# Recurrence of a two-block network: products with the values issued ahead of their waits, and constant products between the steps of a triangular inverse

## The reference, cut to what matters

```python
def first_block(x, ...):
    x = x + FFN_HALF * swiglu(rms_norm(x, norm_ffn1[l]), ...)
    h = rms_norm(x, norm_mix[l])
    p = h @ w_in[l]
    sb_q, sb_k, sb_v, rw_in = jnp.split(p, [...], axis=-1)
    ...
    o_sb = stick_breaking_attention(q, k, v)
    o_sb = rms_norm(o_sb, sb_out_norm[l].reshape(SB_HEADS, HEAD_DIM)).reshape(B, S, SB_WIDTH)
    o_rw = rwkv7_time_mix(rw_in, ...)      # y = rwkv7_recurrence(r, heads(decay), kf, v, -kk, kk * a)
    x = x + jnp.concatenate([o_sb, o_rw], axis=-1) @ w_out[l]
    x = x + FFN_HALF * swiglu(rms_norm(x, norm_ffn2[l]), ...)
```

## Time and profile before

| | |
|---|---|
| time, median of 3 runs | 1114.93 us (1114.87, 1114.93, 1120.08) |
| time of the profiled execution | 1117.52 us |
| its span in the trace | 1115.7 us, so 1.8 us lie around it |
| PE busy | 1088.8 us, 98% of the span |
| DVE, ACT, POOL busy | 670.3, 448.1, 35.6 us |
| chain that ended last | PE 89%, DVE 6%, ACT 4% |
| mean granted TensorE clock | 0.987 of full speed |

### The profile page before, as it was taken

How to read it: one execution, slowest core, us unless ns; L and a number is a source line. 1 busy time by engine, 2 the same in 40 slices (tenths; PEclk the granted TensorE clock), 3 DMA queues, 4 the chain that set the end, 5 groups by cost and what they waited for, 6 DMA issues and landing times.

```text
span 1115.7 us, 19112 instructions
## 1 busy us (share of the span) xinstructions
PE 1088.8 (98%) x8212; PEld 896.2 (80%) x8212; DVE 670.3 (60%) x848; ACT 448.1 (40%) x573; POOL 35.6 (3%) x29
## 2 busy tenths in 40 slices
PE   9999999999998999999999999999999999999997
PEld 8999998999987669999998999989899753434343
DVE  6488777789554666777775573277559552222123
ACT  6333334864522244333335332267584521211112
POOL 0000000000430000000003000000000000000000
PEclk9999999999978999999999999999999999999999
DMA  9977756354200248598873353332356979999994
GB/s 333 390 257 238 251 188 206 119 175 148 90 2 2 76 140 314 190 337 295 306 265 114 96 184 110 108 118 104 114 192 264 375 319 402 422 410 419 422 418 201
DMA packets 121012, 254.29 MB, mean 228 GB/s; under 512 B 6241, under 2 KB 91505, under 8 KB 109426
## 3 DMA queue, kind: packets, MB, share of 16 engines
q1 hardware_dynamic: 119890, 250.54, 61.6%
q10 hardware_dynamic: 1056, 2.79, 0.8%
HBM read 252.25 MB, written 1.06 MB: 227 GB/s over the span
## 4 chain that ended last, share of the span: by engine, by line
PE 89%; DVE 6%; ACT 4%; issue 1%; DMA 0%; SPq 0%; ACTq 0%; DVEq 0%
PE ps L825 53%; PE ps L772 33%; ACT arena L1563 2%; DVE ring_r L2130 1%; ACT arena_r L1563 1%; DVE ring_r L2263 1%; PE ps L1308 1%; DVE arena L2451 1%; DVE arena L2317 1%; DMA x<-in_x 0%; DVE arena L2332 0%; PE ps L793 0%; ACT gb_r L1563 0%; PE ps L1513 0%; PE ps L781 0%
## 5 line engine op out<-in xcount | busy, mean ns | idle before, releaser
L825 PE MATMUL ps<-hall_r,arena_r 128*128 128x256 f32 x1632 | 299.6, 281 | 0.0
L825 PE MATMUL ps<-arena_r 128*128 128x256 f32 (+1 forms) x1216 | 284.4, 323 | 0.0
L2130 DVE TENSOR_TENSOR ring_r<-ring,arena_r 128x2048 fp32r<-128x2048 f32 x88 | 203.1, 2312 | 109.1 <-ACT arena_r L1563 106.6
L825 PEld LDWEIGHTS ps<-hall_r,arena_r 128*128 128x128 f32 x1632 | 252.8, 188 | 1.2 <-issue 0.3
L1563 ACT ACTIVATE arena_r<-ring 128x2048 fp32r<-128x2048 f32 (+1 forms) x101 | 191.1, 1899 | 150.3 <-PE ps L825 139.9
L825 PE MATMUL ps<-hall_r,ring_r 128*128 128x256 f32 x816 | 227.9, 279 | 0.0
L825 PEld LDWEIGHTS ps<-arena_r 128*128 128x128 f32 x1216 | 202.7, 188 | 18.9 <-issue 0.7
L772 PE MATMUL ps<-arena 64*64 64x32 f32 (+7 forms) x1944 | 195.8, 331 | 11.2 <-ACT arena L1563 5.0
L1563 ACT ACTIVATE arena<-ps 128x512 f32<-128x512 f32 (+3 forms) x136 | 80.4, 605 | 312.6 <-PE ps L825 186.2
L772 PEld LDWEIGHTS ps<-arena 128*64 128x64 f32 (+3 forms) x1944 | 117.8, 154 | 71.1 <-issue 58.6
L825 PEld LDWEIGHTS ps<-hall_r,ring_r 128*128 128x128 f32 x816 | 154.9, 190 | 0.9
(11 more groups left out here) (273 smaller groups left out, 1137.8 us busy)
## 6 DMA issues: line engine op xcount, KB each, us to landing
ring<-in_w_in SPq DMA_DIRECT2D x35, 1024.0 KB, 5.2
arena<-in_w_exp_down SPq DMA_DIRECT2D x32, 1024.0 KB, 11.8
ring<-in_ffn_up SPq DMA_DIRECT2D x22, 1024.0 KB, 5.3
ring<-in_ffn_down SPq DMA_DIRECT2D x22, 1024.0 KB, 5.0
ring<-in_ffn_gate SPq DMA_DIRECT2D x21, 1024.0 KB, 5.7
arena<-in_w_mod SPq DMA_DIRECT2D x18, 1024.0 KB, 9.3
arena<-in_w_exp_up SPq DMA_DIRECT2D x16, 1024.0 KB, 14.5
ring<-in_w_exp_gate SPq DMA_DIRECT2D x16, 1024.0 KB, 11.4
```

The source lines that it names most:

```text
L825: m = pe.matmul(out_, w[i], h[j], start=start and i + j == 0, stop=stop and j == 1, skip_group_check=group)
L2130: tt(lo(n), slot(n), hi(n), ALU.subtract).then_inc(S("w_lo"), 1)
```

## The change

The products of the recurrence that need only the values are split from the others. For chunk 0 the right side (`rec_rhs_v(0)`) is issued before the attention's mean squares; for the others it is issued at the end of the chunk before. The state's products with the values are issued in the wait for ACT's copy (for chunk 0 in the wait for DVE's), those of y in the wait for DVE's copy (for chunk 0 in the wait for the inverse). The state's sums move from bank 4 to bank 7. Two constant products of 128x128 weights with 256 columns (`keep_running`) are added at five places of the inverse, and one such product twice in a chunk. ACT copies `rhs_z` of chunk 0 before it copies the attention's output and takes the root. DVE's `sb_out(c)` comes after the state of chunk c, and the fourth after chunk 3. `rhs_z` moves from arena block 20 to block 4, and POOL clears its block and that of `u_z` by two commands that wait on earlier events.

```diff
-        rhs_z, u_z = (A(j).rearrange("p (q n) -> p q n", q=2) for j in (20, 21))
+        rhs_z, u_z = (A(j).rearrange("p (q n) -> p q n", q=2) for j in (4, 21))
...
-            pool.wait_ge(*W("inv_x", 5))
-            pool.memset(A(20, 2048), 0.0).then_inc(S("u_zero"), 1)
+            pool.wait_ge(*W("sb_z", 4))
+            pool.memset(A(4), 0.0).then_inc(S("u_zero"), 1)
+            pool.wait_ge(*W("inv_x", 4))
+            pool.memset(A(21), 0.0).then_inc(S("u_zero"), 1)
...
+            def rec_rhs_v(c):
+                for h in range(8):
+                    m = mm(ps[rec_rows(c), 0, h * CH:(h + 1) * CH], ak_t[:, 8 * (c // 2) + h, :],
+                           vz[:, c % 2, c // 2, h * HD:(h + 1) * HD], start=h == 0, stop=c == 0, group=True)
+                if c == 0:
+                    m.then_inc(S("rec_rhs"), 1)
+
+            def rec_rhs_state(c):
+                for h in range(8):
+                    m = mm(ps[rec_rows(c), 0, h * CH:(h + 1) * CH], arz[:, h % 2, h // 2, c, 0, :],
+                           state[:, c % 2, h // 2, :], start=False, group=True)
+                m.then_inc(S("rec_rhs"), 1)
+
+            def rec_state_v(c):
+                for h in range(8):
+                    o = ps[(h % 2) * HD:(h % 2 + 1) * HD, 7, (h // 2) * HD:(h // 2 + 1) * HD]
+                    mm(o, k_tok[:, c // 2, h * HD:(h + 1) * HD],
+                       vz[:, c % 2, c // 2, h * HD:(h + 1) * HD], start=h < 2, stop=False, group=True)
+
+            def rec_state_u(c):
+                for h in range(8):
+                    o = ps[(h % 2) * HD:(h % 2 + 1) * HD, 7, (h // 2) * HD:(h // 2 + 1) * HD]
+                    m = mm(o, b_tok[:, c // 2, h * HD:(h + 1) * HD],
+                           u_z[:, c % 2, h * HD:(h + 1) * HD], start=False, group=True)
+                m.then_inc(S("rec_state"), 1)
+
+            def rec_y_v(c):
+                if c >= 2:
+                    pe.wait_ge(*W("y_kept", c - 1))
+                for h in range(8):
+                    mm(rec_y_at(c, h), vz[:, c % 2, c // 2, h * HD:(h + 1) * HD],
+                       rk_t[:, 8 * (c // 2) + h, :], start=h < 2, stop=False, group=True)
+
+            def rec_y_u(c):
+                for h in range(8):
+                    m = mm(rec_y_at(c, h), u_z[:, c % 2, h * HD:(h + 1) * HD],
+                           rb_t[:, 8 * (c // 2) + h, :], start=False, stop=c == 0, group=True)
+                if c:
+                    for h in range(8):
+                        m = mm(rec_y_at(c, h), state[:, c % 2, h // 2, :], arz[:, h % 2, h // 2, c, 1, :],
+                               start=False, group=True)
+                m.then_inc(S("rec_y"), 1)
+
+            def keep_running():
+                for i in range(2):
+                    mm(ps[:, 7, 0:256], zeros[:, 0:P], zeros)
+
...
             inv_sums(1)
+            keep_running()
             inv_update(1)
+            keep_running()
             inv_sums(2)
+            keep_running()
             inv_update(2)
             sb_sums_a(0)
             sb_sums_a(1)
             inv_sums(3)
+            keep_running()
             inv_update(3)
...
             inv_sums(5)
             pe.wait_ge(*W("sb_expo", 4))
+            pe.wait_ge(*W("rec_masked", 3))
+            rec_rhs_v(0)
             pe.wait_ge(*W("sbo_sq", 2))
             four(4, lambda o, k: mm(o, head_mean, sq[:, k, :]), "sbo_ms")
+            keep_running()
             inv_update(5)
...
             for c in range(NCH):
...
                 if c:
                     pe.wait_ge(*W("state", c))
...
+                    rec_rhs_state(c)
+                if 0 < c < NCH - 1:
+                    rec_state_v(c)
+                if c == 0:
+                    pe.wait_ge(*W("sb_kept", 1))
+                    rec_y_v(c)
+                    pe.wait_ge(*W("tt_added", 5))
                 pe.wait_ge(*W("rhs_kept", c + 1))
...
                 m.then_inc(S("rec_u"), 1)
+                if c == 0:
+                    rec_state_v(c)
+                else:
+                    rec_y_v(c)
+                mm(ps[:, 6, 0:256], zeros[:, 0:P], zeros)
                 pe.wait_ge(*W("u_kept", c + 1))
...
                 if c < NCH - 1:
...
+                    rec_state_u(c)
+                rec_y_u(c)
+                if c < NCH - 1:
+                    rec_rhs_v(c + 1)
+                    mm(ps[:, 6, 0:256], zeros[:, 0:P], zeros)
...
-            f(mix[0], banks(2), ACT.Copy).then_inc(S("sb_kept"), 1)
-            act.wait_ge(*W("sbo_ms", 2))
-            f(kn, banks(4), ACT.Sqrt, bias=EPS_COL).then_inc(S("sbo_root"), 1)
...
                 f(rhs_z[rows_, c % 2, :], ps[rows_, 0, :], ACT.Copy).then_inc(S("rhs_kept"), 1)
+                if c == 0:
+                    f(mix[0], banks(2), ACT.Copy).then_inc(S("sb_kept"), 1)
+                    act.wait_ge(*W("sbo_ms", 2))
+                    f(kn, banks(4), ACT.Sqrt, bias=EPS_COL).then_inc(S("sbo_root"), 1)
...
-            sb_out(0)
...
-                    sb_out(c + 1)
+                sb_out(c)
+            v.wait_ge(*W("sb_out", 4))
```

More of the change, by code:

```diff
@@ L179, in build @@
             "pool_all": [("c_zero", 2), ("selectors", 2), ("reset_ones", 1), ("reset_mask", 1), ("inv_0", 4),
-                         ("level_a", 5), ("u_zero", 1), ("gates_biased", 4), ("w_zero", 1)],
+                         ("level_a", 5), ("u_zero", 2), ("gates_biased", 4), ("w_zero", 1)],
             "pool_rec": [("rec_masked", 3), ("x_zero", 1)],
@@ L1138, in inv_update, with rec_rows @@
                 m.then_inc(S("inv_t"), 1)
+            def rec_rows(c):
+                return slice((c % 2) * CH, (c % 2 + 1) * CH)
+            def rec_rhs_v(c):
[9 more added lines that the diff above has]
+                m.then_inc(S("rec_rhs"), 1)
@@ new lines, in rec_y_at @@
+            def rec_y_at(c, h):
+                return ps[(h % 2) * HD:(h % 2 + 1) * HD, 2 + c % 2, (h // 2) * CH:(h // 2 + 1) * CH]
+            def rec_y_v(c):
[13 more added lines that the diff above has]
+                m.then_inc(S("rec_y"), 1)
@@ L1157, in _ @@
             pe.wait_ge(*W("sb_expo", 4))
+            pe.wait_ge(*W("rec_masked", 3))
+            rec_rhs_v(0)
             pe.wait_ge(*W("sbo_sq", 2))
             four(4, lambda o, k: mm(o, head_mean, sq[:, k, :]), "sbo_ms")
+            keep_running()
             inv_update(5)
-            pe.wait_ge(*W("rec_masked", 3))
             for c in range(NCH):
-                t, base = c // 2, (c % 2) * CH
-                rows_ = slice(base, base + CH)
-                pe.wait_ge(*W("tt_added", 5))
@@ L1176, in _ @@
+                if c == 0:
+                    pe.wait_ge(*W("sb_kept", 1))
+                    rec_y_v(c)
+                    pe.wait_ge(*W("tt_added", 5))
                 pe.wait_ge(*W("rhs_kept", c + 1))
                 for h in range(8):
-                    m = mm(ps[rows_, 1, h * CH:(h + 1) * CH], inv_tt[:, 8 * t + h, :],
+                    m = mm(ps[rec_rows(c), 1, h * CH:(h + 1) * CH], inv_tt[:, 8 * (c // 2) + h, :],
                            rhs_z[:, c % 2, h * HD:(h + 1) * HD])
@@ L1180, in _ @@
                 m.then_inc(S("rec_u"), 1)
+                if c == 0:
[3 more added lines that the diff above has]
+                mm(ps[:, 6, 0:256], zeros[:, 0:P], zeros)
                 pe.wait_ge(*W("u_kept", c + 1))
-                if c == 0:
-                    pe.wait_ge(*W("sb_kept", 1))
-                    pe.wait_ge(*W("sbo_root", 1))
                 if c < NCH - 1:
[L1186 to L1199, removed]
@@ L1200, in _ @@
-                m.then_inc(S("rec_y"), 1)
+                    rec_state_u(c)
[3 more added lines that the diff above has]
+                    mm(ps[:, 6, 0:256], zeros[:, 0:P], zeros)
             pe.wait_ge(*W("y_kept", 4))
@@ L1833, in _ @@
                 act.wait_ge(*W("rec_rhs", c + 1))
-                act.wait_ge(*W("u_zero", 1))
+                act.wait_ge(*W("u_zero", 2))
                 f(rhs_z[rows_, c % 2, :], ps[rows_, 0, :], ACT.Copy).then_inc(S("rhs_kept"), 1)
+                if c == 0:
+                    f(mix[0], banks(2), ACT.Copy).then_inc(S("sb_kept"), 1)
+                    act.wait_ge(*W("sbo_ms", 2))
+                    f(kn, banks(4), ACT.Sqrt, bias=EPS_COL).then_inc(S("sbo_root"), 1)
                 act.wait_ge(*W("rec_y", c + 1))
@@ L2423, in _ @@
                 v.wait_ge(*W("rec_u", c + 1))
-                v.wait_ge(*W("u_zero", 1))
+                v.wait_ge(*W("u_zero", 2))
                 v.tensor_copy(u_z[rows_, c % 2, :], ps[rows_, 1, :]).then_inc(S("u_kept"), 1)
@@ L2427, in _ @@
                     v.wait_ge(*W("rec_state", c + 1))
-                    sums = ps[:, 4, 0:256].rearrange("p (k n) -> p k n", k=4)
+                    sums = ps[:, 7, 0:256].rearrange("p (k n) -> p k n", k=4)
                     if c:
```

## The result

The changed kernel takes 1109.07 us (median of 5 runs, 1108.59 to 1110.73); the kernel before took 1118.07 beside it (5 runs, 1114.87 to 1120.08). The medians lie 9.0 us apart; the ratio is 0.9935, 95% interval 0.9912 to 0.9957, which is about 7 us, where the prediction said 10.9 and started from 1114.93. The profiled execution of the changed kernel took 1110.73 us, its span 1108.9 against 1115.7.

The account below looks back on a forecast made before the run. TensorE was taken to bound the kernel, with 13.6 and 10.2 us at half clock. Gains of 5.3 (inverse), 0.3 (up to u of chunk 0) and 5.3 (chunks) sum to 10.9: 1114.93 becomes 1104.0 us, range 1101 to 1109.5.

Parts of the forecast that it names:

- B: Rival: the second slow stretch, behind inv_update(5) and into the recurrence, stays; 1107.7 us; chance 0.11.
- C: Rival: fillers don't hold the clock, in the inverse (1110.9 us, chance 0.05) or in both stretches (1114.6 us, chance 0.06).
- D: Rival: slower, the clock falls and doesn't return in the recurrence, period 10.0 us for three chunks; 1123 us; chance 0.04.
- A: The forecast itself: both slow stretches, in the inverse and the recurrence, go; 1104.0 us; chance 0.74.
- the stretch at 323 with large products near holds: Inverse: after small products and 0.70 us idle, with 256-column products shortly ahead, the clock holds; evidence that short fillers hold it.
- I charge 0.1 for each of the first four: Inverse: each of the first four keep_running pairs, 0.96 us, nearly fits its wait and costs 0.1 us.
- What is late next would be DVE ... hidden by 1.6 us: Inverse: DVE's softplus ends at 311.51, needed only by the second half of sb_sums_a at about 313.1; costs nothing.
- Part 2: From the start of four to rec_u(0): 7.07 us becomes 6.76, 0.3 gained, the filler there costing its whole 0.96.
- `rec_y_v` and a filler, 0.98, fill the 0.98: Chunks, in DVE's wait between rec_u and rec_state_u: these products cost nothing; 0.5 us a chunk if alternation were lost.
- costs its 0.48: End of a chunk: PE's products, not DVE, set the pace, so this filler costs 0.48 us; period 6.66.
- The shift is kept: From y_mean on, PE, ACT and DVE do as before and loads wait on PE, so the 10.9 us gain stays.
- the gaps of 0.88 us would not have dropped the clock: The skill's HAM oscillation section as read: only longer DMA waits drop the clock, so closing these gaps wouldn't raise it.

Follow-up runs that it names:

- the order alone: Changed kernel with all constant products taken out, the new order kept: 1111.56 us, ratio to before 0.9952; profiled a second time at 1108.86 us.
- second profile of before: The kernel before, unchanged, profiled in one more execution: 1114.71 us.
- the run with single products: Changed kernel with one constant product instead of two in four waits of the inverse, none elsewhere: 1104.49 us, ratio to before 0.9897.
- the inverse alone: Changed kernel with the five pairs of constant products in the inverse kept and both in the chunk taken out: 1108.1 us, ratio to before 0.9924.
- the last two variants: Changed kernel with one constant product in four waits of the inverse, none elsewhere: 1104.49 us; the same with last_vectors_turned in two parts: 1104.78 us.
- the two variants with the split: last_vectors_turned issued in two parts with a product of keys between: in the changed kernel 1109.61 us; with single constant products in four waits 1104.78 us.
- the small-products kernel: Changed kernel with each keep_running made of 32 products of 64x64 weights with 32 columns: 1112.99 us, ratio to before 0.9976.

## Why the prediction was off

The direction and the mechanism of the inverse were right, the size wasn't: 0.65% in place of 1.0%. Of the rivals B, C and D none came; the clock is full from 300 to 373 us, as in A. The 1109.07 us lie inside the stated 1101 to 1109.5, but by luck: that range was widened for B, which didn't come. The step that failed is the price of the constant products, too low by 1.8 us in the chunks and by 0.6 in the inverse, and with it the gain in the clock that they were to bring the chunks. Point by point:

- **The constant products hold the clock in the inverse: right.** The granted clock is 1.00 throughout, and without them it fell in each of four profiles (two of before, two of the order alone). Products of zeros kept it up.
- **"the stretch at 323 with large products near holds": true of one execution.** The second profile of before and the first of the order alone lost the clock there, at 324.4 and 324.7 us. So this row was no support for the conclusion, which is right.
- **"I charge 0.1 for each of the first four": too little.** In the three waits for ACT a pair costs 0.3 (0.95 less 0.65), and in the wait for DVE 0.1. The term was 0.4 and measured 1.0. The product's own price is higher here: 0.63 us for the first one behind 64-wide weights, and 0.43 for a second (1.06 less 0.63), where the prediction took 0.48 each from the mean squares, whose weights are all 128 wide. The fifth pair stands behind just those and took 0.96 (336.25 to 337.21), as predicted. One product in place of two removes the cost in the waits, as the run with single products shows.
- **"What is late next would be DVE ... hidden by 1.6 us": the margin was gone.** DVE's softplus ended not at 311.5 but at 313.35, and `sb_sums_a` waited for it at 313.37; it took 3.95 us, where the prediction had 3.84 and the kernels with single products, DVE being in time, have 3.65. The last section says what held DVE up.
- **Part 2: right**, 0.36 against 0.3, and with it that the fifth pair isn't hidden: without it the part is 5.73 us, 0.86 less.
- **"`rec_y_v` and a filler, 0.98, fill the 0.98", and the end-of-chunk filler "costs its 0.48": this is the step that failed.** The first costs 0.25 us in each of four chunks, the second 0.76 in each of three. That is 1.0 + 3 x 0.28 = 1.8 more than priced. The order itself did 0.3 better than priced: 22.63 less three fillers of 0.48 is 21.19, and 20.93 is measured. Together 24.22 in place of 22.63. The prediction's own sign of this came: a distance of 7 or more at full clock, 7.10.
- **What the prediction didn't ask: whether the recurrence needs them at all.** It took the slow 10.2 us of one profile for a property of the kernel, and 3.3 of its 5.3 us from them. The second profile of before hasn't got them, and five profiles of the new order without constants in the chunks (two of the order alone, the inverse alone, and the last two variants) keep the clock there; what the executions that weren't profiled did isn't shown. So in the chunks the constants cost 24.22 - 20.93 = 3.3 us. Against the second profile of before, the chunks gain only 24.56 - 24.22 = 0.34: the order's 3.6 us (24.56 less 20.93) is paid back almost whole by the constants put beside it.
- **"The shift is kept": true of the waits, not of the clock.** Nothing new waits from `y_mean` on, up to 612 us the lead is whole. Then the clock fell for 3.4 us in the profiled execution, 1.92 us lost. It does so in part of the executions of several kernels: in four of the eleven profiles that have the turn in one piece, the two of before not among the four. All four have the new order, of which there are eight; of the three in the old order none has it. So this fall comes and goes between executions of one kernel (the changed one has it in one profile and not in the other), but whether the change makes it likelier is open.
- **"the gaps of 0.88 us would not have dropped the clock".** The prediction read this from the section on HAM oscillation of the Trainium skill, "TensorE: Matmul & The Clock Gate", which speaks of longer gaps. With no gap above 0.88 us the clock fell in four profiles of four, and with constant products in these gaps in none of nine, so for this kernel the runs decide against that reading.
- **What stays open.** The time of before is spread over 6 us; two profiles show that falls of the clock differ by 6.8 us in length, worth 2.65 us of the stretch; the rest of the spread is not traced. Of the measured gain some 3 us thus depend on which executions of before are drawn. That the group of 4-column instructions makes the late fall rests on its place and on the two variants with the split, one profile each, not on a run that made it always fall; seven profiles have the group in one piece and no fall behind it. Whether one constant product per wait is always enough rests on two profiles and 12 times.

The best version, one product in each of four waits and none elsewhere, takes 1104.49 us, 4.6 us less than the changed kernel. Its 5.46 us in the stretch are the sum of the prices above: 3.3 in the chunks, 0.86 ahead of the last step, 1.0 for the second product of the pairs, 0.3 in `sb_sums_a`.

## What to carry to other kernels

Work that only keeps the clock up must be shorter than the wait it stands in, measured with the weights that stand around it, and must stand in waits alone; first take it out place by place, for denser real work may hold the clock by itself. Before a slow stretch of a profile is priced, take a second profile: the clock of this kernel fell for 10.2 us of the recurrence in one execution and not at all in the next. And follow a lead won in one stage to the end of the program: here 1.9 us of it went 250 us later.

## What the runs showed of the hardware

**A busy PE can lose its clock.** Ahead of the late fall PE has no idle time at all. It does 32 instructions of 4 columns, at 65 ns each, on the timeline of the changed kernel:

```profile
610.42 2.08 PE L774 MATMUL ps<-cst,hall 128*64 128x4 f32 x32
```

The clock was at 0.50 from 613.0; in the order-alone kernel the group started at 612.16 and the fall came at 614.8, in the one with single products at 605.06 and 607.5. Yet 64 instructions of 32 columns in a row, one group after another, held it for 11 us (302.2 to 313.5) in the small-products kernel. The Trainium skill, "TensorE: Matmul & The Clock Gate", Part 1, has the clock follow how busy TensorE has been; if that is read as the profile's busy time, the trace doesn't agree, for it was 1.00 in every window from 605 to 613 us.

**The same products, two rates.** 64-wide products that alternate between two halves of the partitions take 31 ns an instruction, and those into one half 58; the new order keeps both rates.

**DVE held up by POOL.** A product of two on-chip buffers on DVE took 0.69 us in the kernel before and 2.41 in the changed one. DVE's and POOL's timelines of the kernel before:

```profile
308.41 0.69 DVE L2366 TENSOR_TENSOR arena<-arena,cst 128x512 f32<-128x512 f32 x1
```

```profile
308.59 4.78 POOL L721 TENSOR_TENSOR arena<-arena,cst 128x1024 f32<-128x1024 f32 x2
```

and the changed one:

```profile
308.53 2.41 DVE L2417 TENSOR_TENSOR arena<-arena,cst 128x512 f32<-128x512 f32 x1
```

```profile
308.39 4.41 POOL L721 TENSOR_TENSOR arena<-arena,cst 128x1024 f32<-128x1024 f32 x2
```

Where DVE starts first, it takes 0.69 us; where POOL's first product has begun, DVE's lasts until 310.8 to 311.1. All ten profiles looked at follow this, with 0.69 in four and 1.74 to 2.41 in six; in the four, POOL's two products take 4.8 us in place of 4.4. The Trainium skill, "SBUF — State Buffer", section "SBUF: two separate sides", says that a VectorE operation with two inputs in this memory and a GpSimd operation that reads it exclude each other for a whole instruction, and the trace agrees. Here it took the whole margin of 1.6 us and cost 0.3 of the path (3.95 in `sb_sums_a` against 3.65).
